# Gate halves before up halves in two of the three units of each expert body

## The reference, cut to what matters

```python
D_MODEL, N_EXPERTS_2, EXPERT_HIDDEN = 1024, 16, 512      # every row goes to 2 of the 16 experts
def hier_moe_2(x, w_group, b_group, w_expert, b_expert, w_gate, w_up, w_down):
    ...
    y = jnp.zeros_like(t)
    for e in range(N_EXPERTS_2):
        h = jax.nn.silu(t @ w_gate[e]) * (t @ w_up[e])
        y = y + gates[:, e:e + 1] * (h @ w_down[e])
```

## Time and profile before

| | |
|---|---|
| time, median of 3 runs | 1604.29 us (1600.18 to 1609.49) |
| time of the profiled execution | 1601.46 us |
| its span (first to last instruction) | 1599.8 us |
| PE busy | 1430.4 us, 89% of the span, mean granted clock 0.95 |
| first unit of body 0 starts at | 1276.52 us |
| starts of bodies 1 to 7 | 1318.72, 1356.40, 1394.25, 1431.66, 1470.56, 1508.26, 1545.56 us |

### The profile page before, as it was taken

One profiled execution on the slowest core, in us unless ns is written; L12 is line 12 of the kernel. 1 busy time (PEld: TensorE's weight loads), 2 busy tenths in 40 slices (PEclk: granted clock), 3 DMA queues, 4 the chain that ended last, 5 costly groups with the idle time before them and its releaser, 6 DMA issues. The chain is left out here.

```text
span 1599.8 us, 23287 instructions
## 1 busy us (share of the span) xinstructions
PE 1430.4 (89%) x10284; PEld 738.3 (46%) x10284; DVE 439.5 (27%) x816; ACT 358.8 (22%) x613; POOL 171.5 (11%) x243
## 2 busy tenths in 40 slices
PE   5989999887799999999789999776989799999996
PEld 3434444577545545544344444465545543333332
DVE  2233405442324111111621000693522300000015
ACT  2024016444223011111321100322433111111112
POOL 5000003254000200000000000240000201111100
PEclk8989999999999899999999999985999899999999
DMA  6261100200064599999702210000232468999984
GB/s 198 96 225 52 53 0 0 107 4 4 10 233 167 207 415 416 418 418 416 305 23 109 79 54 0 1 1 1 106 138 115 186 274 331 354 359 371 350 343 158
DMA packets 73483, 283.83 MB, mean 177 GB/s; under 512 B 14145, under 2 KB 15496, under 8 KB 61090
## 3 DMA queue, kind: packets, MB, share of 16 engines
q1 hardware_dynamic: 66368, 267.47, 43.1%
q0 software_dynamic: 5440, 10.58, 1.9%
q10 hardware_dynamic: 1570, 4.24, 0.7%
HBM read 259.41 MB, written 29.84 MB: 181 GB/s over the span
## 5 line engine op out<-in xcount | busy, mean ns | idle before, releaser
L346 PE MATMUL banks<-mixT,ring 128*128 128x512 f32 x672 | 292.9, 598 | 0.8 <-DVE mixT L2481 0.8
L346 PEld LDWEIGHTS banks<-mixT,ring 128*128 128x128 f32 x672 | 128.8, 192 | 164.3 <-issue 163.0
L2171 PE MATMUL banks<-arena_moe,mixT 128*32 128x512 f32 x768 | 170.5, 595 | 0.0
L2171 PE MATMUL banks<-ring,mixT 128*32 128x512 f32 x768 | 113.9, 603 | 15.2 <-DMA arena_moe<-in_w_up 10.9
L1454 PE MATMUL banks<-ring,mixT 128*128 128x512 f32 x256 | 116.6, 611 | 7.5 <-PEq L50 4.9
L1730 PE MATMUL banks<-G_moe,x_hi_moe 128*128 128x256 f32 (+1 forms) x320 | 82.8, 297 | 4.9 <-DVE G_moe L1772 2.6
L343 PE MATMUL banks<-ring,mixT 128*128 128x512 f32 x192 | 82.9, 592 | 0.0
L1730 PE MATMUL banks<-G_moe,x_lo_moe 128*128 128x256 f32 (+1 forms) x320 | 81.1, 292 | 0.0
L1755 DVE TENSOR_TENSOR mixT<-banks,params 128x512 f32<-128x512 f32 (+1 forms) x64 | 40.0, 625 | 146.8 <-PE banks L1730 83.4
L1454 PEld LDWEIGHTS banks<-ring,mixT 128*128 128x128 f32 x256 | 48.9, 196 | 65.5 <-issue 65.5
L2171 PEld LDWEIGHTS banks<-ring,mixT 128*32 128x32 f32 x768 | 36.2, 111 | 89.6 <-issue 85.1
(11 more groups left out here) (429 smaller groups left out, 1981.3 us busy)
## 6 DMA issues: line engine op xcount, KB each, us to landing
ring<-in_w_in SPq DMA_DIRECT2D x18, 1024.0 KB, 7.6
arena_moe<-in_exp_w_gate SPq DMA_DIRECT2D x16, 1024.0 KB
arena_moe<-in_exp_w_up SPq DMA_DIRECT2D x16, 1024.0 KB
arena_moe<-in_exp_w_down SPq DMA_DIRECT2D x16, 1024.0 KB, 16.8
ring<-in_exp_w_gate SPq DMA_DIRECT2D x16, 1024.0 KB, 12.9
ring<-in_exp_w_up SPq DMA_DIRECT2D x16, 1024.0 KB, 15.5
ring<-in_exp_w_down SPq DMA_DIRECT2D x16, 1024.0 KB, 17.9
arena_moe<-in_w_gate SPq DMA_DIRECT2D x8, 2048.0 KB
```

What stands on the lines that cost most here:

```text
L346: last = pe.matmul(bank[:], w[:, c, i * P:(i + 1) * P], m.mixT[:, c, :], start=(c == 0), stop=(c == DC - 1))
L2171: last = pe.matmul(hb[u][T * i:T * (i + 1), :], z.xe[:, j, at:at + T], both[:, :, j, half * 256:half * 256 + 256], start=(j == 0), stop=(j ...
```

## The change

Unit 0 stays as it is. Units 1 and 2 of each body are computed by a new function: first all eight chunks of the gate halves (256 moving columns each), then all eight of the up halves. A new semaphore `gates` is raised when a gate half is complete. SP waits for it, and asks for the next body's gate weights of that expert then; the up weights are asked for where both were before. What is computed, the number of DMAs, their sizes and their order are the same.

```diff
-    def load_in(self, sp, io, s, body, sem):
+    def load_in(self, sp, io, s, body, sem, parts=(0, 1)):
 
         both, _ = self.expert(s) if self.wide else self.slot(s)
-        for k in range(2):
+        for k in parts:
             w = self.weights_of(io, self.weights[k], body * self.EB + s)
             sp.dma_start(both[:, k], w.rearrange("(p c) n -> p c n", p=P)).then_inc(sem, 16)
...
             for s in range(2):
+                sp.wait_ge(ph.sem("gates"), 2 * i + s - 1)
+                z.load_in(sp, io, s, i, ring[s], (0,))
                 sp.wait_ge(ph.sem("hidden"), 3 * i + s - 1)
-                z.load_in(sp, io, s, i, ring[s])
+                z.load_in(sp, io, s, i, ring[s], (1,))
...
+        def gates_before_ups(i, u):
+
+            for part in range(2):
+                for j in range(DC):
+                    for k, (s, half) in enumerate(tiles[u]):
+                        both, _ = z.expert(s)
+                        at = T * k if u < 2 else P + T * (k % 2)
+                        last = pe.matmul(hb[u][T * k:T * (k + 1), 256 * part:256 * part + 256], z.xe[:, j, at:at + T],
+                                         both[:, part, j, half * 256:half * 256 + 256], start=(j == 0), stop=(j == DC - 1),
+                                         skip_group_check=True)
+                last.then_inc(ph.sem("gates" if part == 0 else "hidden"), 1)
...
         def body(i):
             gate_up(ph, i, 0, ring)
-            gate_up(ph, i, 1, ring)
+            gates_before_ups(i, 1)
             turn_hidden(ph, i, 0)
-            gate_up(ph, i, 2, ring)
+            gates_before_ups(i, 2)
             turn_hidden(ph, i, 1)
```

## The result

| | before | after |
|---|---|---|
| median of 6 runs | 1604.24 us (1600.18 to 1611.13) | 1590.86 us (1589.11 to 1592.93) |
| ratio to before, 95% interval | | 0.9913 [0.989, 0.9936] |
| profiled execution, span | 1601.46, 1599.8 | 1590.82, 1589.1 |
| PE busy | 1430.4 us | 1428.7 us |

The change made the kernel 0.87% faster. I had forecast 1596.8 us and a range down to 1591; the time lies just under it, and the forecast of "within 0.5%" was wrong.

The account below looks back on a forecast made before the run. PE was taken as nearly the bound, the DMA engines nearly too, with 10.9 us of PE idle. Gains of 8.3, less end bodies' cost and 0.4, gave 7.5: 1594.0 profiled, 1596.8 us median, range 1591 to 1606.

Parts of the forecast that it names:

- within 0.5%: Whole kernel: a time within about 8.0 us of before, which a measurement can't tell from no change; chance 0.52.
- rival 1: Second expert stage: the last DMA engine sets the end, so only 1.5 us is gained, 1602.8 us; chance 0.18.
- rival 2: Second expert stage: all 10.9 us of PE's wait goes and short groups cost nothing, 1593.4 us; chance 0.08.
- rival 3: The 512 short groups: weight loads come out from under matmuls, 0.13 us a group, 1660 us; chance 0.06.
- its second form: Units 1 and 2: PE can't issue records so densely, at 71 ns a record 1629 us; chance 0.03.
- rival 4: Early gate request: it comes no earlier or waits behind another, only the 1.5 us cost shows, 1605.8; chance 0.03.
- the sum: Second expert stage: smaller of PE and DMA idle per body, 8.3 us, less end bodies' cost and 0.4, gives 7.5.
- the two tightest: Second expert stage: 0.4 us taken off by choice, as engines finish apart and not all idle time is usable.
- The short matmuls: Units 1 and 2: 256-column groups cost 0.09 us a unit, 1.5 us for 16 units (0 to 2.9).
- the lower bound: Units 1 and 2: a 256-column group takes half of 0.4285, 0.2143 us, so no cost at all.
- the row with two strips: L737, 256 columns on two strips: second group starts 0.22 us after the first; upper bound, 0.18 us more a unit.
- the median 2.8 us above it: Whole kernel: runs' median lies 2.8 us above the profiled execution, taking the forecast from 1594.0 to 1596.8 us.

Follow-up runs that it names:

- run 10: The change, but gate weights are asked for after half the up half, 1.7 us before the up request instead of 3.45: 1594.38 us, 0.9928 of before.
- run 7: The change with columns cut once more, 128 per matmul and 256 records a unit, same requests: 1632.1 us, 1.0213 of before.
- runs 5 and 6: Kernel before, then changed kernel, each never loading gate and up weights of bodies 1 to 7: 1586.22 us (0.9922) and 1582.37 us (0.9909).
- run 4: The kernel before, unchanged, for a second profile and more runs: 1606.82 us, 1.0009 of before.
- the second set: The changed kernel, unchanged, run again beside the kernel before on one chip: 1592.5 us, 0.9926 of before.
- runs 3 and 12: Run 12, and before it the change with only expert 1's gate weights asked for early: 1604.67 us, 0.9996 of before.
- run 12: The change plus the same edit in the first expert stage, both units in halves with early gate requests: 1593.64 us, 0.9938 of before.
- run 11: The 128-column kernel of run 7 with gate and up weights of bodies 1 to 7 never loaded: 1606.04 us, 0.9997 of before.
- runs 1 and 10: Run 10, and the changed kernel's halved units with all weight requests where they were before: 1604.37 us, 0.9992 of before.
- runs 4 and 9: Run 4, and the changed kernel, unchanged, measured again: 1592.5 us, 0.9926 of before.

## Why the prediction was right or wrong

**The mechanism was right.** PE's wait for the last up transfer was what there was to win, the request for expert 0's gate was where it was won, SP's order did not stand in its way, and PE's own work is what binds next. Of the rivals, the last DMA engine (rival 1) is refuted by run 10 and by the waits that are gone; rival 2, "all of the wait goes and the short groups cost nothing", is what happened but for the 0.41 us in body 4, with 0.08 given to it; loads and issue (rival 3) do not show, but its second form is nearer than I thought, as run 7 shows; rival 4 did not occur. Units of 128 records in 6.91 us, and run 7's 256 in 6.99, are 54 and 27 ns a record. The 62 ns a matmul that the Trainium skill gives for decoding in software ("TensorE: Matmul & The Clock Gate", "Wait — 56ns, not 53.3ns?") would have made them 7.94 and 15.9 us; by the trace that limit does not bind here. Which way of decoding these runs had is not shown.

**The step that failed** is in the sum: "Per body the smaller of (PE's idle time - 0.18) and the DMA engines' idle time". I took a body's DMA share as its need. It is not: the queue is a backlog, and the window from one body start to the next holds packets that were asked for in the body before, while the next body's spill out of it. Body 4 had 0.97 x 38.90 = 37.7 us of DMA work in its window before and has 36.3 now. The whole stretch shows that the work is the same. Before and after, bodies 1 to 6 together:

```profile
1318.72:1545.56 226.84, 215.97 (x1860) 75.02 (x1853) 21.76 (x44) 25.81 (x55) 22.01 (x22) 1.00 0.93 356
```

```profile
1318.99:1535.00 216.01, 215.60 (x2632) 98.06 (x2628) 21.76 (x44) 25.09 (x54) 22.02 (x22) 1.00 0.98 374
```

0.93 x 226.84 = 211 us of DMA work before, 0.98 x 216.01 = 212 after: 35.2 and 35.3 a body, under PE's 35.9. Done over the stage, the same bound would have cut nothing off. Done by body, it took 1.5 us from body 4 (the smaller of 2.69 and 1.17), and the 0.4 for "the two tightest" went with it. What the run took there was 0.41, the wait that is left.

**The term that was mis-sized** weighs as much. The short matmuls: 1.5 us expected, 0.6 by runs 5 and 6; the lower bound, half of 0.4285, was nearly the truth, and the row with two strips and a rounded 0.22 was a poor guide. The sum also left out that units behind a wait take 0.2 us more, which goes with the wait: over the six bodies PE's busy time fell by 0.4 us (215.97 to 215.60), where the sum had it rise by 1.1. The six bodies became 226.84 - 216.01 = 10.8 us shorter, where the sum had 8.3 - 0.4 = 7.9; the profiled span fell by 10.7, where it had 7.5. Of these 3.2 us the bound and the 0.4 make about 1.5, the matmuls the rest. One reading was off without weight in the sum: the transfers take up to 17.01 us (body 4), not "16 us at most".

**The median.** I set the profiled execution's gain against the median 2.8 us above it. The kernel after has its median at its profiled execution (1590.86 and 1590.82), so 2.7 us of the 13.4 between the medians is not in the pair of profiles. A part may go with the waits, which differ between executions (10.9, 12.4, 11.4 and 9.9 us in the four profiles that have them); once in these four, and once in run 10, the clock fell after one, for 1.7 us. That this makes up the 2.7 is not shown, since the same fall also comes without them (run 4), and the start of the stage moves by more. By the second set (0.9926, 13.0 us between the medians, [0.9914, 0.9938]) a gain of 10.7 us, 0.9933, lies within both intervals, and the forecast's 7.5, 0.9953, in neither.

**The chances.** "Within 0.5%" had 0.52 because the sum came out at 7.5 with the limit at 8.0. It followed from the step above; with the bound taken over the stage the sum is 10.9 - 1.5 = 9.4, and faster would have been the likeliest. The forecast of the median would have been 1594.9 even so; that the measured 1590.86 lies 5.9 us under the 1596.8 is 3.2 of the sum and 2.7 of the medians.

## What to carry to other kernels

Where a transfer queue did not run dry, asking earlier bought no time (runs 3 and 12); look for the place where its engines' share dips, and move the one request that follows the dip. Half of the lead could not be told from the whole. A wait that goes is worth nothing if another stands behind it, as in run 12. Bound a stage by the DMA work of the whole stage, not of each iteration's window, because a backlog carries over. And before halving matmuls, count instructions as well as columns.

## What the runs showed of the hardware that was not expected

- Instructions have a rate of delivery. Under full DMA load PE got 16 KB, which are 256 instructions or 128 load and matmul pairs, once in 6.2 us (run 7: 3.70 us of work, 2.51 us of standing still), and once in about 3.4 to 4.3 us with the engines mostly free (run 11). Groups of four float32 matmuls on 32-column strips with 256 columns need a packet each 6.9 us and ran without a stall; with 128 columns they need one each 3.5 and did not.
- Loads of 32 columns on four strips keep up with groups of 0.109 us: 256 records in 6.99 us (run 7, unit 1).
- After waits of 2.89 and 1.98 us the granted clock fell to 1.2 GHz for a time (runs 1 and 10, 1.7 us lost each), after one of 2.87 us it did not (kernel before). Behind the same wait of 1.87 or 1.88 us in the last body the first down unit took 7.08 us in the first profile of each kernel, and 8.75 and 8.77 in the second (runs 4 and 9).
